# High and low halves of standing weights written element by element in turns

## The chip, the cores and the metric

The kernel runs on one core of one Trainium2 chip. The metric is device time in microseconds, from the start of the program to its end on that core.

## What is computed

The reference runs one network made of two blocks over 256 tokens of width 1024, all in fp32. Cut to what matters for the change:

```python
for l in range(2):                         # first block
    h, hc = norm(x) * (1 + sc1) + sh1, ... # latent tokens and context tokens
    u = h @ w_glu; q, k, v = h @ w_q, h @ w_k, h @ w_v; p = h @ w_p
    g = sigmoid(h @ w_g + b_gate)          # three gates of width 1024
    y = (g0 * y_a + g1 * y_b + g2 * y_c) @ w_out
    x = x + (silu(h2 @ w1) * (h2 @ w3)) @ w_ffn_out   # hidden width 2816
for i in range(2):                         # second block, on the same x
    x = x + concat(mixer(norm(x) @ w_in), memory) @ w_out
    x = x + (silu(g) * u) @ w_down         # g, u = split(norm(x) @ w_gate_up)
out = norm(x)
```

The first layer of the first block treats 256 latent and 256 context tokens together (512 columns), its second layer mostly the 256 latent ones, and the second block 256 tokens. Nearly all of the time goes into products of activations with weight matrices that are read once from memory.

## The kernel before, in words

The program is written engine by engine, with semaphores between the engines. `build` lays out the memory by hand; the first block is `block1`, the second `block2`.

To keep precision, each fp32 matrix is held as two fp32r halves: a high half, rounded, and a low half, the rest. `multiply` (L345 to L349) makes a product of three matmuls: first operand's high with second's high (L347), high with low (L348), low with high (L349). The first operand of a matmul stands still in the array and is fetched by a weight load of 128 x 128; the second moves through it.

Weights come in chunks of 1024 elements a partition. `T.load` (L256) books a chunk. SP's queue (`load_chunks`) brings it into the ring `raw` (3 buffers in the first block, 5 in the second). ScalarE copies it to the high half (L333), VectorE takes the high half off the raw chunk and so makes the low half (L336). Both do this in `split_until`, in the order in which TensorE uses the chunks, up to two chunks ahead. TensorE waits for `low_done` before it uses a chunk. A buffer of the split ring is filled again once TensorE has reported the last product that used it (`T.used`, `split_free`).

A split buffer is `[P, 2, SLOT]`: 1024 high elements, then 1024 low elements. The first block has 3 of them, the second 4. In the first block each exists twice over nearly the same memory: `level`, which starts at a multiple of 256 bytes as the activations HH and HL do, and `apart`, 64 bytes (`APART`) further. The second block has one set, 64 bytes past a multiple of 256. `T.load` chooses by the number of moving columns:

```python
two = rings[b][1 if columns > SEQ else 2][(len(old) - now["split"]) % SPLIT[b]]
```

Weights are used in two ways. Where the output is wanted with channels on the partitions, the weights stand still and the activations HH and HL move, 256 or 512 columns wide. This is so in `product_t`, `half_by_half`, `ffn_pe`, `raw_ffn_pe`, the gates and branches of the first block and the memory keys of the second. A chunk is then one output tile of 128 channels with 8 slices of the inner dimension (4 slices for two of the branches), so it takes 8 x 3 matmuls. A slice of the weights is 128 elements, 512 bytes, side by side. In `product` it is the other way round: the weights move, 512 or 256 columns wide, and the activations stand still.

In the profile, an operand pair such as `HH,apart` names the moving tile first and the standing one second; `split` is the `level` set in the first block and the only set in the second.

Of the kernel before, what the change touches and what calls it, by code (L numbers as in the profile page):

```python
# [123 lines left out]
def build(nc, A, out):  # L124
# [97 lines left out]
    class Tensor:  # L222
# [30 lines left out]
                milestones[key] = bank_no[1]  # L253
            ins.then_inc(pe_done, 1)

        def load(self, src, shape, split=True, ring="raw", home_free=None, split_home=None, later=False, columns=2 * SEQ):  # L256


            b = now["block"]
            mine = in_ring[ring]  # L260
            size = RAW[b] if ring == "raw" else MOD_RING
            s = (len(mine) - now[ring]) % size
            pieces = src if isinstance(src, list) else [src]
            loads[ring][s] += 16 * len(pieces)
            home = rings[b][0][s][:, :] if ring == "raw" else G[:, s, :]
            c = {"pieces": pieces, "shape": shape, "sem": slot_full[ring][s], "raw": view(home, shape), "full": loads[ring][s],
                 "free": None, "split": None, "before": mine[-size] if len(mine) - size >= now[ring] else None,
                 "mods": len(in_ring["mod"]) - len(held), "home_free": home_free}
            if later:
                held.append(c)  # L270
            else:
                chunks.append(c)
                chunks.extend(held)
                held.clear()
            mine.append(c)
            if not split:
                self.pe.wait_ge(c["sem"], c["full"])
                return c, c["raw"]
            k = c["split"] = len(splits)
            if split_home:  # L280
                two, c["split_free"] = split_home
            else:
                old = in_ring["split"]
                two = rings[b][1 if columns > SEQ else 2][(len(old) - now["split"]) % SPLIT[b]]
                c["split_free"] = old[-SPLIT[b]] if len(old) - SPLIT[b] >= now["split"] else None
                old.append(c)
            c["high"], c["low"] = view(two[:, 0, :], shape), view(two[:, 1, :], shape)
            splits.append(c)
            self.pe.wait_ge(low_done, k + 1)
            return c, (c["high"], c["low"])  # L290
# [16 lines left out]
    def view(t, shape):  # L307
        a, b = shape
        return t[:, 0:a * b].rearrange("p (a b) -> p a b", a=a)
# [51 lines left out]
    def product_t(T, pe, name, w, c0, tiles, kts, rhs, n, source=None, before=None, fill=None):  # L361

        per = SLOT // kts // P
        for j in range(tiles):
            if j % per == 0:
                src = source(j) if source else rows(w, 0, kts, c0 + j * P, per * P)
                i, ws = T.load(src, (kts, per * P), columns=n)
            if before:
                before(j)
            tile_t(T, pe, (name, j), ws, kts, j % per, rhs, n)  # L370
            if j % per == per - 1:
                T.used(i)
            if fill:
                fill(j)
# [703 lines left out]
    def half_by_half(T, pe, name, tiles, key, source, turned=0):  # L1078

        norm_pe(T, pe, name, tiles, turned, max(turned, 2))  # L1080
        norm_wait(pe, name, tiles[0:2])
        ws = {}
        for h in range(2):
            to = slice(h * SEQ, (h + 1) * SEQ)
            for p in range(3):
                if h == 0:
                    ws[p] = T.load(source(p), (KT, P), columns=SEQ)
                    T.open(key(p))
                for k in range(KT):
                    ins = multiply(pe, bank(key(p))[:, to], cut2(ws[p][1], slice(None), k), (HH[:, k, to], HL[:, k, to]), k == 0, k == KT - 1)  # L1090
                if h == 0 and p < 2:
                    norm_pe(T, pe, name, tiles, max(turned, 2 + p), 3 + p)
                elif h:
                    T.close(ins, key(p))
                    T.used(ws[p][0])
            if h == 0:
                norm_wait(pe, name, tiles)

    def ffn_pe(T, pe, L, w_up, w_down, tiles, n, U, wait, fill=nothing, down=nothing, last=1, homes=None, after_part=None):
        skip = 3 if len(tiles) > 2 else 0  # L1100
        parts = ("ffn_gate", 0), ("ffn_up", D_FF)
        if skip:
            half_by_half(T, pe, L + "n2", tiles, lambda p: (L + parts[p % 2][0], p // 2),
                         lambda p: rows(w_up, 0, KT, parts[p % 2][1] + p // 2 * P, P), 2)
        else:
            norm_pe(T, pe, L + "n2", tiles)
            keep_busy(T, pe, WARM_LAST[L + "n2"])
            wait(pe, L + "n2", tiles)
        for j in range(FT):
            for nm, c0 in parts:  # L1110
                if 2 * j + (nm == "ffn_up") < skip:
                    fill(2 * j + (nm == "ffn_up"))
                    continue
                i, ws = T.load(rows(w_up, 0, KT, c0 + j * P, P), (KT, P), columns=n)
                tile_t(T, pe, (L + nm, j), ws, KT, 0, both((HH, HL), n), n)
                T.used(i)
                fill(2 * j + (nm == "ffn_up"))
        product(T, pe, L + "ffn", w_down, FT, D, tiles, lefts(U), before=lambda k: pe.wait_ge(S(L + "hidden"), k + 1), fill=down, last=last,
                homes=homes, after_part=after_part)
# [86 lines left out]
    def _(pe):  # L1206
# [24 lines left out]
        for l in range(DEPTH):  # L1231
# [12 lines left out]

            for j in range(4):
                if j >= skip:
                    i, ws = T.load(rows(w_in, 0, KT, COL_P + j * P, P), (KT, P), columns=n)
                    tile_t(T, pe, (L + "pool", j), ws, KT, 0, own, n)
                    T.used(i)
                mod_pe(T, pe, L + "proj", j)  # L1250
                if j == 3 and l == 0:
                    for m in range(2):
                        turn_params(stage[1][:, m, :], ("cols", 1, m), 1)
                if j < 2 and first == 2:
                    norm_pe(T, pe, L + "n1", [0, 1, 2, 3], 2 + j, 3 + j)
            for j in range(NCH):
                for nm, c0 in glus:
                    i, ws = T.load(rows(w_in, 0, KT, c0 + j * P, P), (KT, P), columns=n)
                    tile_t(T, pe, (L + nm, j), ws, KT, 0, own, n)
                    T.used(i)  # L1260
                    mod_pe(T, pe, L + "proj", 4 + 2 * j + (nm == "glu"))
# [113 lines left out]

            def branch(name, number, gate_col, w, kts, pair, ready):
                for j in range(KT):
                    i, ws = T.load(rows(w_in, 0, KT, COL_G + gate_col * D + j * P, P), (KT, P), columns=n)
                    tile_t(T, pe, (name + "_gate", j), ws, KT, 0, own, n)
                    T.used(i)  # L1380
                    if number == 0 and l == 0 and j == 1:
                        conv_mean()
                    if number == 0 and l == 0 and j == 3:
                        conv_var()
                    if j == 0:
                        ready()
                    iy, wy = T.load(rows(w, 0, kts, j * P, P), (kts, P), columns=n)
                    tile_t(T, pe, (name, j), wy, kts, 0, both(pair, n), n)
                    T.used(iy)
                    if number == 1:  # L1390
                        gate_pe(T, pe, l, 0, j - 2)
# [823 lines left out]
    def raw_ffn_pe(T, pe, L, w_up, w_down, U, down):  # L2215

        raw_rows_pe(T, pe, L + "n2", 1)
        keep_busy(T, pe, BUSY_LAST)
        norm2_wait(pe, L + "n2", [0, 1])
        for j in range(FT):  # L2220
            for nm, c0 in (("ffn_gate", 0), ("ffn_up", D_FF)):
                i, ws = T.load(rows(w_up, 0, KT, c0 + j * P, P), (KT, P))
                tile_t(T, pe, (L + nm, j), ws, KT, 0, both((HH, HL), SEQ), SEQ)
                T.used(i)
                if j == 0 and nm == "ffn_gate":
                    spread_pe(T, pe, L + "n2")
        product(T, pe, L + "ffn", w_down, FT, D, [0, 1], lefts(U), before=lambda k: pe.wait_ge(S(L + "hidden"), k + 1), fill=down, last=2)
# [37 lines left out]
    def _(pe):  # L2265
# [3 lines left out]
        for e in range(DEPTH):  # L2269
# [56 lines left out]
            def next_memory(i):  # L2326
# [16 lines left out]
                if n < 2:  # L2343
                    key = ("E1_km", n)
                    if h == 0:
                        mem_chunks[n] = T.load(rows(w, 0, KT, n * P, P), (KT, P))
                        T.open(key, FILL_BANK)
                    c, ws = mem_chunks[n]
                    for k in range(4 * h, 4 * h + 4):
# [431 lines left out]
```

## Time and profile before

| | us |
|---|---|
| three runs | 2254.14, 2245.88, 2249.35 |
| median | 2249.35 |
| the profiled execution | 2247.56 |
| its span, first to last instruction | 2245.8 |
[...]

The profile shows one execution. PE are matmuls and PEld the weight loads beside them. A matmul's record holds its whole passage through the array, longer than the interval to the next one, so the pace is read from counts in windows without idle time, not from the mean of one. Where the rows give a mean, a longer one for the same form still says that it was held up.

### The profile page before, as it was taken

The numbers are of one execution on the slowest core, as the hardware profiler recorded it, in microseconds if no ns is written. First come the engines' busy times: TensorE is split into PE (matmuls) and PEld (weight loads), VectorE is DVE, ScalarE is ACT, GpSimd is POOL, SyncE is SP. The second block draws the span as 40 slices with busy tenths as digits, with TensorE's granted clock in tenths as the row PEclk, the third lists the DMA queues.
The fourth block names the chain that finished last, engine by engine and source line by source line (L and its number), as shares of the span: only waits on it lengthen the run. The fifth ranks groups of instructions, "written<-read, shape, count | busy, mean of one in ns | idle before, by whom it ended". The sixth has DMA issues, their size and how long they took to land. (4 is left out here: it accounts for less than half of the span.)

```text
span 2245.8 us, 32948 instructions
## 1 busy us (share of the span) xinstructions
PE 2160.7 (96%) x13134; PEld 1870.9 (83%) x13134; DVE 1444.3 (64%) x2148; ACT 888.4 (40%) x1389; POOL 179.5 (8%) x251
## 2 busy tenths in 40 slices
PE   5999999999999999999999999999999999999998
PEld 3777667878888888788886998998888998898997
DVE  3587685664467667237967776874785665566664
ACT  3322373332342212235327545443544444444443
POOL 3422000000000000004310001000100000000000
PEclk9999999999999999999999999999989999999999
DMA  8544302333335566234420565776633666543663
GB/s 281 160 141 141 99 1 62 96 97 94 113 103 170 177 197 207 99 116 139 129 75 24 170 181 160 238 215 194 160 113 90 184 187 195 155 130 113 188 196 123
DMA packets 428653, 320.81 MB, mean 143 GB/s; under 512 B 25925, under 2 KB 379702, under 8 KB 428502
## 3 DMA queue, kind: packets, MB, share of 16 engines
q1 hardware_dynamic: 425408, 310.52, 45.8%
q0 software_dynamic: 2656, 8.03, 1.2%
q8 instruction: 105, 1.72, 0.3%
q14 instruction: 46, 0.38, 0.0%
q10 hardware_dynamic: 438, 0.17, 0.0%
HBM read 317.62 MB, written 1.05 MB: 142 GB/s over the span
## 5 line engine op out<-in xcount | busy, mean ns | idle before, releaser
L336 DVE TENSOR_TENSOR split<-raw,split 128x1024 fp32r<-128x1024 f32 (+1 forms) x382 | 460.2, 1209 | 366.8 <-ACT split L333 365.9
L347 PE MATMUL PS<-HH,split 128*128 128x256 f32 (+1 forms) x1752 | 590.9, 337 | 4.1 <-DVE HL L2163 1.7
L349 PE MATMUL PS<-HH,split 128*128 128x256 f32 (+1 forms) x1752 | 580.0, 331 | 0.0
L348 PE MATMUL PS<-HL,split 128*128 128x256 f32 (+1 forms) x1752 | 579.9, 331 | 0.0
L333 ACT ACTIVATE split<-raw 128x1024 fp32r<-128x1024 f32 (+1 forms) x382 | 389.1, 1033 | 359.8 <-PE PS L349 324.4
L347 PEld LDWEIGHTS PS<-HH,split 128*128 128x128 f32 x1752 | 331.3, 189 | 42.2 <-issue 9.0
L348 PEld LDWEIGHTS PS<-HL,split 128*128 128x128 f32 x1752 | 334.1, 191 | 32.0 <-issue 1.0
L349 PEld LDWEIGHTS PS<-HH,split 128*128 128x128 f32 x1752 | 331.0, 189 | 31.6
L347 PE MATMUL PS<-HH,apart 128*128 128x256 f32 x800 | 227.0, 284 | 17.8 <-DVE HL L487 11.8
L348 PE MATMUL PS<-HL,apart 128*128 128x256 f32 x800 | 223.2, 279 | 0.0
L349 PE MATMUL PS<-HH,apart 128*128 128x256 f32 x800 | 223.1, 279 | 0.0
L336 DVE TENSOR_TENSOR apart<-raw,apart 128x1024 fp32r<-128x1024 f32 x118 | 136.4, 1162 | 69.4 <-ACT apart L333 68.8
L347 PEld LDWEIGHTS PS<-HH,apart 128*128 128x128 f32 x800 | 152.0, 190 | 22.0 <-DVE HL L487 13.3
L347 PE MATMUL PS<-split,UH 128*128 128x512 f32 x416 | 165.3, 397 | 1.4 <-DVE split L336 1.4
L348 PE MATMUL PS<-split,UH 128*128 128x512 f32 x416 | 162.6, 391 | 0.0
L349 PE MATMUL PS<-split,UL 128*128 128x512 f32 x416 | 162.4, 390 | 0.0
L1744 DVE SCALAR_TENSOR_TENSOR CV<-UP,cols,CV 128x512 f32<-128x512 f32 (+1 forms) x240 | 155.1, 708 | 0.2
L348 PEld LDWEIGHTS PS<-HL,apart 128*128 128x128 f32 x800 | 152.0, 190 | 0.2
L349 PEld LDWEIGHTS PS<-HH,apart 128*128 128x128 f32 x800 | 152.1, 190 | 0.0
L333 ACT ACTIVATE apart<-raw 128x1024 fp32r<-128x1024 f32 x118 | 117.4, 999 | 82.6 <-PE PS L349 54.2
L938 DVE SCALAR_TENSOR_TENSOR XN<-G,silu_c,XN 128x1024 f32<-128x1024 f32 x70 | 88.0, 1281 | 36.0 <-ACT UT L1127 35.3
L347 PEld LDWEIGHTS PS<-split,UH 128*128 128x128 f32 x416 | 78.4, 189 | 19.2 <-DVE split L336 2.0
(339 smaller groups left out, 3117.9 us busy)
## 6 DMA issues: line engine op xcount, KB each, us to landing
raw<-in_w_in_dram SPq DMA_DIRECT2D x120, 512.0 KB, 4.2
raw<-in_w_ffn_in_dram SPq DMA_DIRECT2D x88, 512.0 KB, 4.8
raw<-in_l_w_gate_up_dram SPq DMA_DIRECT2D x88, 512.0 KB, 3.9
G<-in_w_mod_dram SPq DMA_DIRECT2D x82, 512.0 KB, 3.9
raw<-in_w_ffn_out_dram SPq DMA_DIRECT2D x44, 512.0 KB, 3.5
raw<-in_l_w_down_dram SPq DMA_DIRECT2D x44, 512.0 KB, 4.5
raw<-in_l_w_in_dram SPq DMA_DIRECT2D x28, 512.0 KB, 3.9
raw<-in_w_attn_out_dram SPq DMA_DIRECT2D x16, 512.0 KB, 4.3
```

The lines of the kernel that those rows point to most:

```text
L333: eng.activation(c["high"], c["raw"], ACT.Copy).then_inc(high_done, 1)
L336: eng.tensor_tensor(c["low"], c["raw"], c["high"].bitcast(F32), ALU.subtract).then_inc(low_done, 1)
L347: pe.matmul(out, a[0], b[0], start=first, stop=False)
L348: pe.matmul(out, a[0], b[1], start=False, stop=False)
L349: return pe.matmul(out, a[1], b[0], start=False, stop=last)
L938: ins = dve.scalar_tensor_tensor(at, c["raw"][:, 0, :], s, at, ALU.mult, ALU.add)
L1744: ins = dve.scalar_tensor_tensor(CV[:, j, 0:ns, :], src, wt, CV[:, j, 0:ns, :], ALU.mult, ALU.add)
```

## The change

`T.load` gets an argument `still` in place of `columns`. For a chunk whose weights stand still, the split buffer is taken from the `apart` set whatever the number of moving columns, and the two halves are laid out in turns: high element 0, low element 0, high element 1, and so on. The high view and the low view then have a step of two elements, 8 bytes. ScalarE writes every second element, VectorE reads and writes every second element, and a weight load reads 128 elements out of 1024 bytes. Chunks that move keep two halves one behind the other, in the `level` set.

```diff
-        def load(self, src, shape, split=True, ring="raw", home_free=None, split_home=None, later=False, columns=2 * SEQ):
+        def load(self, src, shape, split=True, ring="raw", home_free=None, split_home=None, later=False, still=False):
...
-                two = rings[b][1 if columns > SEQ else 2][(len(old) - now["split"]) % SPLIT[b]]
+                two = rings[b][2 if still else 1][(len(old) - now["split"]) % SPLIT[b]]
...
-            c["high"], c["low"] = view(two[:, 0, :], shape), view(two[:, 1, :], shape)
+            if still:
+                a, n = shape
+                pairs = two.rearrange("p o (n h) -> p (o n) h", h=2)
+                c["high"], c["low"] = (pairs[:, 0:a * n, h].rearrange("p (a n) -> p a n", a=a) for h in range(2))
+            else:
+                c["high"], c["low"] = view(two[:, 0, :], shape), view(two[:, 1, :], shape)
...
-                i, ws = T.load(src, (kts, per * P), columns=n)
+                i, ws = T.load(src, (kts, per * P), still=True)
...
-                i, ws = T.load(rows(w_up, 0, KT, c0 + j * P, P), (KT, P), columns=n)
+                i, ws = T.load(rows(w_up, 0, KT, c0 + j * P, P), (KT, P), still=True)
```

The same last edit is made in `half_by_half`, at the pool and gated-unit tiles, at the gates and branches of the first block, in `raw_ffn_pe` and at the memory keys: everywhere weights stand still.

## Rows read from the trace of the kernel before

**Rows 1.** Busy time, share of the span and instructions of each engine, from the page.
```profile
PE 2160.7 (96%) x13134; PEld 1870.9 (83%) x13134; DVE 1444.3 (64%) x2148; ACT 888.4 (40%) x1389; POOL 179.5 (8%) x251
```

**Rows 2.** TensorE's waits: us in total, times, longest.
```profile
PE PS L347 <- DVE HL L487: 11.8, 4, 8.3
...
PE PS L347 <- DVE apart L336: 7.1, 7, 3.2
...
PE PS L347 <- DVE split L336: 1.4, 1, 1.4
...
PE PS L703 <- DVE split L336: 0.9, 1, 0.9
```

**Rows 3.** Matmuls in windows: length, busy us (count), granted clock, DMA share, GB/s.
```profile
1410.00:1480.00 70.00, 70.00 (x620) 1.00 0.82 246
1780.00:1850.00 70.00, 70.00 (x597) 1.00 0.65 188
2100.00:2170.00 70.00, 70.00 (x596) 1.00 0.65 186
955.00:990.00 35.00, 35.00 (x156) 1.00 0.34 107
```

**Rows 4.** Forms in the windows 1410:1500 (`apart`) and 1770:1890 (`split`): busy, mean ns.
```profile
L348 PE MATMUL PS<-HL,apart 128*128 128x256 f32 x260 | 71.8, 276 | 0.0
...
L348 PEld LDWEIGHTS PS<-HL,apart 128*128 128x128 f32 x260 | 48.8, 188 | 0.0
...
L348 PE MATMUL PS<-HL,split 128*128 128x256 f32 x294 | 82.6, 281 | 0.0
...
L348 PEld LDWEIGHTS PS<-HL,split 128*128 128x128 f32 x294 | 56.4, 192 | 0.0
```

**Rows 5.** Weight loads in order of time, 1484.5:1485.7: start, length.
```profile
1484.33 1.31 PEld L917 LDWEIGHTS PS<-ones,XN 128*128 128x128 f32 x11
1485.56 0.19 PEld L347 LDWEIGHTS PS<-HH,apart 128*128 128x128 f32 x1
```

**Rows 6.** Matmuls by form, whole span: count, busy, mean ns.
```profile
L348 PE MATMUL PS<-HL,split 128*128 128x512 f32 x784 | 307.8, 393 | 0.0
...
L348 PE MATMUL PS<-HL,split 128*128 128x256 f32 x968 | 272.1, 281 | 0.0
...
L348 PE MATMUL PS<-HL,apart 128*128 128x256 f32 x800 | 223.2, 279 | 0.0
...
L348 PE MATMUL PS<-OTL,apart 128*128 128x256 f32 x64 | 18.5, 289 | 0.0
```

**Rows 7.** Matmuls by form in the windows 1000:1595 and 400:450.
```profile
L348 PE MATMUL PS<-HL,apart 128*128 128x256 f32 x704 | 195.6, 278 | 0.0
...
L348 PE MATMUL PS<-HL,split 128*128 128x512 f32 x48 | 18.7, 389 | 0.0
```

**Rows 8.** The two split lines: their forms, then their busy time in two windows.
```profile
L333 ACT ACTIVATE split<-raw 128x1024 fp32r<-128x1024 f32 x363 | 377.0, 1053 | 359.8 <-PE PS L349 324.4 <-DVE X L2174 8.9 <-DMA raw<-in_w_in_dram 8.2
...
L336 DVE TENSOR_TENSOR split<-raw,split 128x1024 fp32r<-128x1024 f32 x363 | 446.6, 1234 | 324.0 <-ACT split L333 323.1
...
1410.00:1480.00 70.00, 27.52 (x26) 1.00 0.82 246
...
1410.00:1480.00 70.00, 31.12 (x26) 1.00 0.82 246
1780.00:1850.00 70.00, 29.66 (x25) 1.00 0.65 188
```

**Rows 9.** All engines in two windows: PE, PEld, DVE, ACT, POOL, granted clock, DMA share, GB/s.
```profile
1410.00:1500.00 90.00, 90.00 (x796) 90.00 (x796) 73.53 (x105) 39.73 (x50) 0.00 (x0) 1.00 0.79 233
1770.00:1890.00 120.00, 120.00 (x955) 117.22 (x954) 79.74 (x119) 50.15 (x63) 0.00 (x0) 1.00 0.65 192
```

**Rows 10.** VectorE in order of time, 1780:1790, with the idle time before.
```profile
1782.50 1.22 DVE L336 TENSOR_TENSOR split<-raw,split 128x1024 fp32r<-128x1024 f32 x1 [1.43 <-ACT split L333]
1783.64 0.41 DVE L2246 TENSOR_TENSOR UT<-UT,PS 128x256 f32<-128x256 f32 x1
1784.09 0.30 DVE L340 CAST UH<-UT 128x256 fp32r<-128x256 f32 x1
1784.42 0.42 DVE L341 TENSOR_TENSOR UL<-UT,UH 128x256 fp32r<-128x256 f32 x1
1784.76 1.22 DVE L336 TENSOR_TENSOR split<-raw,split 128x1024 fp32r<-128x1024 f32 x1
```

More of the change, by code:

```diff
@@ L1086, in half_by_half @@
                 if h == 0:
-                    ws[p] = T.load(source(p), (KT, P), columns=SEQ)
+                    ws[p] = T.load(source(p), (KT, P), still=True)
                     T.open(key(p))
@@ L1246, in _ @@
                 if j >= skip:
-                    i, ws = T.load(rows(w_in, 0, KT, COL_P + j * P, P), (KT, P), columns=n)
+                    i, ws = T.load(rows(w_in, 0, KT, COL_P + j * P, P), (KT, P), still=True)
                     tile_t(T, pe, (L + "pool", j), ws, KT, 0, own, n)
@@ L1257, in _ @@
                 for nm, c0 in glus:
-                    i, ws = T.load(rows(w_in, 0, KT, c0 + j * P, P), (KT, P), columns=n)
+                    i, ws = T.load(rows(w_in, 0, KT, c0 + j * P, P), (KT, P), still=True)
                     tile_t(T, pe, (L + nm, j), ws, KT, 0, own, n)
@@ L1377, in branch @@
                 for j in range(KT):
-                    i, ws = T.load(rows(w_in, 0, KT, COL_G + gate_col * D + j * P, P), (KT, P), columns=n)
+                    i, ws = T.load(rows(w_in, 0, KT, COL_G + gate_col * D + j * P, P), (KT, P), still=True)
                     tile_t(T, pe, (name + "_gate", j), ws, KT, 0, own, n)
@@ L1386, in branch @@
                         ready()
-                    iy, wy = T.load(rows(w, 0, kts, j * P, P), (kts, P), columns=n)
+                    iy, wy = T.load(rows(w, 0, kts, j * P, P), (kts, P), still=True)
                     tile_t(T, pe, (name, j), wy, kts, 0, both(pair, n), n)
@@ L2221, in raw_ffn_pe @@
             for nm, c0 in (("ffn_gate", 0), ("ffn_up", D_FF)):
-                i, ws = T.load(rows(w_up, 0, KT, c0 + j * P, P), (KT, P))
+                i, ws = T.load(rows(w_up, 0, KT, c0 + j * P, P), (KT, P), still=True)
                 tile_t(T, pe, (L + nm, j), ws, KT, 0, both((HH, HL), SEQ), SEQ)
@@ L2345, in next_memory @@
                     if h == 0:
-                        mem_chunks[n] = T.load(rows(w, 0, KT, n * P, P), (KT, P))
+                        mem_chunks[n] = T.load(rows(w, 0, KT, n * P, P), (KT, P), still=True)
                         T.open(key, FILL_BANK)
```

## Prediction

> **What bounds the kernel now.** I read the shares of the engines first. The reader is to see that TensorE is busy for 96% of the span and its weight loads for 83%, VectorE for 64% and ScalarE for 40% [rows 1]. The table of waits by engine comes next: TensorE waits 7.1, 1.4 and 0.9 us for a low half, which is all the time in which it stood for want of split weights [rows 2]. So the order of work ends with TensorE, and the change counts by what it does to the pace at which weight loads and matmuls follow each other.
>
> That pace I read from windows without any idle time. Two matmuls at most are already under way where a window opens, so I take two off each count. The 70 us from 1410 (second layer's hidden layer, 256 moving columns, loads from `apart`) hold 618 matmuls, 113.3 ns each. The 70 us from 1780 and from 2100 (same shapes, second block) hold 595 and 594, 117.7 ns each [rows 3]. Nothing in the instruction differs. The same form takes 276 ns there and 281 ns here, and one of the three loads in a turn takes 192 instead of 188 ns [rows 4]. So there are two paces, and the slow one costs 4.4 ns a matmul. With 512 moving columns, 154 in 35 us give 227 ns, twice the quick pace [rows 3]: 113.3 ns is what 256 moving columns need by themselves.
>
> A weight load has a pace too. Where a matmul has one moving column, eleven loads start in 1485.56 - 1484.33 = 1.23 us, 111.8 ns each [rows 5]. A matmul of 256 columns therefore leaves its load 1.5 ns to spare, one of 512 columns 115 ns. This is the number on which the change hangs.
>
> **The change part by part.** It adds no instruction, wait or transfer, and removes none. No buffer changes its size, and the rings, their counts and the order of SP's queue stay as they are. Three things differ for a chunk whose weights stand still.
>
> (1) Its weight load reads 128 elements out of 1024 bytes instead of 512. How many matmuls that touches: `split` with 256 columns 968 a line, `apart` 800 and 64 a line, over three lines 5496, and the branches of four slices some 200 more (estimated from the loop: 2 x 8 tiles x 4 slices x 3), together 5690 with 256 columns [rows 6]. With 512 columns it is some 2500 (784 a line and the small groups) [rows 6]; there a load may grow by 115 ns before it is felt, and I cost them at nothing.
>
> The trace has no load or other operand that reads every second element, so I bound its price. From below: the load stays at 111.8 ns, and TensorE no longer meets the slow pace. All of the second block's matmuls at the quick one is 3 x 968 x 4.4 ns = 12.8 us. In the first block the mean between 1000 and 1595 is 278 ns, two fifths of the way from 276 to 281, so 3 x 704 x 0.4 x 4.4 = 3.7 us, and 3 x 96 x 4.4 = 1.3 us for the rest if all of it is slow [rows 6, 7]. Together 18 us, as the most that can be had, since 113.3 ns stays the floor of the moving columns and stalls also stand in that mean. From above: the load takes twice its time because it covers twice the bytes, 224 ns, and 5690 x (224 - 113.3) ns - 18 us = 612 us are lost. Between them stands one row. The moving operand covers 1024 bytes in 113.3 ns [rows 3]; a load that reads its 1024 bytes as fast ends just when its matmul does. It is the nearest row, because it is the same engine reading the same length of the same memory, and I take it. Then the load is neither late nor early, and which of the two paces TensorE falls into stays open, as the trace shows no cause for it but how a stretch began. I leave the shares as they are: 0 us, with 18 us of gain and, if all goes at 117.7 ns, 5690 x 4.4 - 18 = 7 us of loss on the two sides.
>
> [...]
>
> [...]
>
> (2) ScalarE writes the high half with gaps, VectorE reads it with gaps and writes the low half with gaps. These splits take 1.05 us (ScalarE) and 1.23 us (VectorE) a chunk [rows 8]. No row has fp32 elements at every second place. Below: no change. Above: both double. I take no change: the nearest rows are the same instructions on a contiguous chunk, and both engines move as many elements as before. What hides them: ScalarE is busy 27.5 of 70 us with splits, VectorE 31.1 of 70 us with splits [rows 8] and 73.5 of 90 us with everything [rows 9]. If the cover is gone, VectorE needs 73.5 + 90 / 70 x 31.1 = 113.5 us in those 90, that is 26% longer, and 79.7 + 120 / 70 x 29.7 = 130.6 in the 120 us of the second block, 9% longer [rows 9]. The stretches last 22 pairs of chunks, 5.44 us a pair (48 x 113.3) and twice 5.65 us, so 22 x (5.44 x 0.26 + 2 x 5.65 x 0.09) = 53 us.
>
> (3) Chunks with 512 moving columns move from `level` to `apart`, 64 bytes further. At 227 ns they are at the floor of their moving columns with either [rows 3], and their means of 393 ns against the floor's 389 [rows 6, 7] leave 2500 x 4 ns = 10 us, most of it halved clock and stalls. I take 0.
>
> The sum: 0 + 0 + 0, with the profiled execution at 2247.56 us, of which its span is 2245.8 and 1.8 lie around it. It lies 1.8 us under the median of the three runs, 2249.35. I say 2248.
>
> **The rivals.** 0.5%, 11 us, is about what a measurement of this kernel can tell from no change.
> A: freed. Weights and moving columns now pass through memory at the same pace, 64 bytes apart, so they never meet and the quick pace is the only one. For it: the slow pace exists, and it comes with a longer load [rows 4]. Against it: the first block holds the quick pace for 70 us with loads as they are [rows 3], so distance in memory alone doesn't make the slow one. It gives 2249 - 18 to 2249 - 11, 2231 to 2238 us. More isn't to be had.
> B: the load becomes the bound, in TensorE's 256-column stretches. It decides from 113.3 ns on, 1.5 ns above what it takes now. [...] At 120 ns it is +20 us, 2269. At half as much again, 168 ns, it is 5690 x 54.7 ns - 18 us = +293 us, 2542. Twice is 2861. For it: only 1.5 ns of cover. Against: a moving operand covers as much at 113.3.
> [...]
> C: ScalarE and VectorE slow down, VectorE becomes the bound: up to +53 us, 2302. Against it: idle time before every second split, 1.43 us long [rows 10].
> D: nothing is seen, because 512-column matmuls hide it and 256-column ones keep their mix. This is my forecast.
>
> **How the numbers follow.** D 0.39, A 0.28, B small (from 2260 to 2285) 0.17, B large 0.10, C 0.06. Faster is A, same is D, slower is B and C, 0.33. The range leaves out B large, half of C and the end of A: 2232 to 2280. As cases of both signs hold most of the chance, D's own range is 2240 to 2258.
>
> **What would show it.** In the window of 1410, a form mean of 276 ns and 618 matmuls in 70 us if the load is still hidden. In the second block's hidden layers, 276 instead of 281 ns for A, 281 for D. For B, loads that follow at more than 113.3 ns with matmuls of the same interval, and 512-column matmuls still at 227. For C, means above 1.05 and 1.23 us on the two split lines and waits of TensorE for a low half. I am wrong if the load's own price is not near that of the moving columns, or if weights and columns that pass at the same pace always meet and not never.

## The result and the profile after

| | before | changed |
|---|---|---|
| median, us | 2250.19 (4 runs, 2245.88 to 2254.14) | 2274.32 (4 runs, 2270.03 to 2281.09) |
| the profiled execution, us | 2247.56 | 2281.09 |
| its span, us | 2245.8 | 2279.3 |
| mean granted TensorE clock | 0.985 | 0.982 |

The ratio is 1.0106, with a 95% interval from 1.007 to 1.0142: the changed kernel is slower, by 24 us in the medians, where no change had been forecast. The time lies inside the range, 2232 to 2280. The profiled execution is the longest of its four, 6.8 us above their median; the other three have clocks of 0.985 to 0.987.

In the changed kernel the three matmuls of `multiply` stand in L352, L353 and L354, ScalarE's half of the split in L338 and VectorE's in L341. The shares on the profile's page of the changed kernel, beside [rows 1]:

```profile
PE 2196.7 (96%) x13134; PEld 1916.4 (84%) x13134; DVE 1445.5 (63%) x2148; ACT 920.1 (40%) x1389; POOL 177.8 (8%) x251
```

TensorE grew by 36.0 us, its weight loads by 45.5, ScalarE by 31.7, VectorE by 1.2. So the loss is TensorE's own, and what is left to ask is which matmuls carry it. The same windows as in [rows 3], changed kernel, and ahead of them one in the first layer of the first block, where weights stand still under 512 moving columns:

```profile
420.00:440.00 20.00, 20.00 (x88) 1.00 0.32 93
955.00:990.00 35.00, 35.00 (x156) 1.00 0.30 98
1410.00:1480.00 70.00, 70.00 (x583) 1.00 0.75 224
1780.00:1850.00 70.00, 70.00 (x585) 1.00 0.65 191
2100.00:2170.00 70.00, 70.00 (x585) 1.00 0.63 183
```

The first of these in the kernel before:

```profile
420.00:440.00 20.00, 20.00 (x90) 1.00 0.32 90
```

All 256-column stretches with standing weights now have one pace: 583 to 585 matmuls in 70 us, which less two is 120.1 to 120.5 ns, against 620, 597 and 596. Where weights move (955:990), nothing changed. Under 512 columns 88 matmuls fit where 90 did. The forms of the window 1410:1500 show the load beside its matmul, to be set against 276 and 188 ns in [rows 4] (busy, mean ns; before, all three loads of a turn took 188 ns there):

```profile
L353 PE MATMUL PS<-HL,apart 128*128 128x256 f32 x250 | 70.9, 284 | 0.0
...
L354 PEld LDWEIGHTS PS<-HH,apart 128*128 128x128 f32 x250 | 48.9, 196 | 0.0
```

The whole span by forms, against [rows 6]: 393 became 396 ns with 512 columns, 279 became 286 in the first block, and 281 stayed 281 on this line of the second:

```profile
L353 PE MATMUL PS<-HL,apart 128*128 128x512 f32 x784 | 310.2, 396 | 0.0
...
L352 PE MATMUL PS<-HH,split 128*128 128x256 f32 x968 | 278.1, 287 | 3.1 <-DVE HL L2168 1.7 <-DVE HL L645 0.8 <-DVE RT L713 0.5
...
L353 PE MATMUL PS<-HL,split 128*128 128x256 f32 x968 | 272.2, 281 | 0.0
L353 PE MATMUL PS<-HL,apart 128*128 128x256 f32 x800 | 228.5, 286 | 0.0
```

A mean of one form hides a loss that is spread over the three of a turn, so I took the time from each matmul's start to the next one's from the trace, left out every gap of 135 ns or more (260 ns with 512 columns), which are stalls or the halved clock (a granted clock of 0.50, as from 895.4 to 898.6 us in the kernel before), and summed what is over the floor of 113.3 (226.7) ns:

| matmuls with standing weights | before: mean ns, us over the floor | changed | difference, us |
|---|---|---|---|
| 2784 with 256 columns, first block | 114.3, 2.7 | 120.0, 17.9 | 15.2 |
| 2904 with 256 columns, second block | 117.4, 11.7 | 120.0, 19.1 | 7.4 |
| 2736 with 512 columns | 227.3, 1.6 | 230.5, 10.2 | 8.6 |

That is 31.2 of the 33.5 us by which the two spans differ, and the matmuls whose weights move stay within 0.1 us of where they were. The medians differ by less, 24 us, with an interval from 16 to 32 (0.7 and 1.42% of 2250). The idle time of TensorE shrank from 85.1 to 82.6 us (span less busy), which gives a little back.

The splits in the whole span, changed kernel:

```profile
L338 ACT ACTIVATE split<-raw 128x1024 fp32r<-128x1024 f32 x257 | 276.4, 1099 | 210.6 <-PE PS L354 192.0 <-DVE X L2179 8.9 <-DVE X L2176 4.8
L338 ACT ACTIVATE apart<-raw 128x1024 fp32r<-128x1024 f32 x208 | 239.0, 1151 | 219.2 <-PE PS L354 188.8 <-DMA raw<-in_w_in_dram 21.8 <-DMA raw<-in_w_ffn_in_dram 8.5
...
L341 DVE TENSOR_TENSOR split<-raw,split 128x1024 fp32r<-128x1024 f32 x257 | 313.5, 1225 | 259.9 <-ACT split L338 259.6
```

And TensorE's wait for a low half, from the table of waits (us, times, longest):

```profile
PE PS L352 <- DVE apart L341: 5.9, 6, 3.1
```

ScalarE's copy went from 1053 ns [rows 8] to 1099 and 1151, VectorE's subtraction stayed where it was, and TensorE waits no longer for a low half than in [rows 2]. ScalarE's 32 us are hidden.

### The profile page after: what moved, and what is told of

It is laid out like the page before. It is cut to its first block and busy times, and to the rows that moved or that the text cites. A ratio compares the mean times of both kernels' runs of the same rounds, so it can differ in the third digit from the quotient of the medians.

```text
span 2279.3 us, 32948 instructions
## 1 busy us (share of the span) xinstructions
PE 2196.7 (96%) x13134; PEld 1916.4 (84%) x13134; DVE 1445.5 (63%) x2148; ACT 920.1 (40%) x1389; POOL 177.8 (8%) x251
## 5 line engine op out<-in xcount | busy, mean ns | idle before, releaser
L352 PE MATMUL PS<-HH,apart 128*128 128x256 f32 (+1 forms) x1584 | 550.3, 347 | 17.1 <-DVE HL L492 11.7
L353 PE MATMUL PS<-HL,apart 128*128 128x256 f32 (+1 forms) x1584 | 538.6, 340 | 0.0
L354 PE MATMUL PS<-HH,apart 128*128 128x256 f32 (+1 forms) x1584 | 537.7, 339 | 0.0
L341 DVE TENSOR_TENSOR split<-raw,split 128x1024 fp32r<-128x1024 f32 x260 | 316.0, 1221 | 259.9 <-ACT split L338 259.6
L341 DVE TENSOR_TENSOR apart<-raw,apart 128x1024 fp32r<-128x1024 f32 x240 | 280.5, 1171 | 195.4 <-ACT apart L338 194.7
L338 ACT ACTIVATE split<-raw 128x1024 fp32r<-128x1024 f32 x260 | 278.7, 1095 | 210.6 <-PE PS L354 192.0
L352 PEld LDWEIGHTS PS<-HH,apart 128*128 128x128 f32 x1584 | 312.3, 197 | 52.2 <-DVE HL L492 13.2
L338 ACT ACTIVATE apart<-raw 128x1024 fp32r<-128x1024 f32 x240 | 259.9, 1086 | 223.5 <-PE PS L354 193.1
L353 PEld LDWEIGHTS PS<-HL,apart 128*128 128x128 f32 x1584 | 312.0, 197 | 29.0 <-issue 1.2
L354 PEld LDWEIGHTS PS<-HH,apart 128*128 128x128 f32 x1584 | 312.2, 197 | 28.8
L352 PE MATMUL PS<-HH,split 128*128 128x256 f32 x968 | 278.1, 287 | 3.1 <-DVE HL L2168 1.7
L354 PE MATMUL PS<-HH,split 128*128 128x256 f32 x968 | 273.8, 283 | 0.0
L353 PE MATMUL PS<-HL,split 128*128 128x256 f32 x968 | 272.2, 281 | 0.0
L352 PEld LDWEIGHTS PS<-HH,split 128*128 128x128 f32 x968 | 187.8, 194 | 6.7 <-issue 4.5
L353 PEld LDWEIGHTS PS<-HL,split 128*128 128x128 f32 x968 | 189.2, 195 | 0.2
L354 PEld LDWEIGHTS PS<-HH,split 128*128 128x128 f32 x968 | 188.5, 195 | 0.0
L352 PE MATMUL PS<-split,UH 128*128 128x512 f32 x416 | 165.2, 397 | 1.4 <-DVE split L341 1.4
L353 PE MATMUL PS<-split,UH 128*128 128x512 f32 x416 | 162.5, 391 | 0.0
L354 PE MATMUL PS<-split,UL 128*128 128x512 f32 x416 | 162.4, 390 | 0.0
L352 PEld LDWEIGHTS PS<-split,UH 128*128 128x128 f32 x416 | 78.5, 189 | 19.1 <-DVE split L341 2.0
```

What stands on the lines that cost most here:

```text
L338: eng.activation(c["high"], c["raw"], ACT.Copy).then_inc(high_done, 1)
L341: eng.tensor_tensor(c["low"], c["raw"], c["high"].bitcast(F32), ALU.subtract).then_inc(low_done, 1)
L352: pe.matmul(out, a[0], b[0], start=first, stop=False)
L353: pe.matmul(out, a[0], b[1], start=False, stop=False)
L354: return pe.matmul(out, a[1], b[0], start=False, stop=last)
```

## The experiments

Three theories could give 120 ns. Theory 1: the load of every second element is itself longer than its matmul. Theory 2: load and moving columns meet in memory, in a way that depends on their distance. Theory 3: the splits, writing with gaps, disturb TensorE's reads.

**A table of paces.** A program of its own runs the same pattern of three matmuls a slice with nothing beside it: weights as two contiguous halves (`cols`), in turns (`turns`), in turns by slices of 128 (`slices`), at every third or fourth element, each at several offsets from a multiple of 256 bytes, where the activations lie.

```diff
+        if kind == "c":
+            f = lambda h, k: t[:, 1024 * h + 128 * k:1024 * h + 128 * (k + 1)]
+        elif kind == "s":
+            f = lambda h, k: t[:, 256 * k + 128 * h:256 * k + 128 * (h + 1)]
+        else:
+            v = t.rearrange("p (n h) -> p n h", h={"i": 2, "t": 3, "d": 4}[kind])
+            f = lambda h, k: v[:, 128 * k:128 * (k + 1), h]
```

> A program of its own, with none of the reference's work: TensorE runs four tiles of 8 x 3 fp32r matmuls for each of many layouts of the standing weights (halves one behind the other, in turns by element, in turns by slice of 128, every third and every fourth element), at offsets of 0 to 224 bytes against the moving columns, with 256, 512 and 8 moving columns, each twice. Afterwards ScalarE and VectorE write with and without gaps, alone and beside TensorE. Read is the interval between matmuls. Theory 1 (the load itself takes longer): with 8 moving columns, loads of every second element follow at about 120 ns, against 112 for contiguous ones, and the interval with 256 columns is 120 at every offset; with 512 columns it stays 227. Theory 2 (load and moving columns meet in memory): with 8 columns both follow at 112 ns, with 256 columns the interval depends on the offset, some at 113 and some at 118 to 121, and with 512 columns there are a few ns over 227 for turns alone. Theory 3 (writes of the other engines with gaps disturb TensorE): in this program, turns without other engines run at 113 ns, and above it only beside them. [...] ScalarE's write with gaps some 100 ns longer than 1.05 us in all theories.

Mean ns from start to start with 256 columns, each run of 96 matmuls seen twice with at most 1.5 ns between the two. One of the sixteen second runs, `cols` at 0, fell into the halved clock (0.50) and is left out. The table gives the first:

| offset, bytes | 0 | 32 | 64 | 96 | 128 | 160 | 192 | 224 |
|---|---|---|---|---|---|---|---|---|
| cols | 119.9 | 118.4 | 113.3 | 117.3 | 118.6 | 120.0 | 117.8 | 116.7 |
| turns | 120.1 | 120.0 | 120.0 | 120.7 | 120.0 | 120.0 | 121.7 | 120.0 |

Slices in turns give 120.0 at 0 and 113.4 at 64; every third element gives 173.3, every fourth 235.5. Windows of this program, matmuls: `cols` at 0, `turns` at 0, `cols` at 64, `turns` at 64, every third, every fourth.

```profile
30.00:38.00 8.00, 8.00 (x69) 1.00 0.01 2
42.00:51.00 9.00, 9.00 (x77) 1.00 0.01 2
77.00:86.00 9.00, 9.00 (x81) 1.00 0.01 2
88.00:98.00 10.00, 10.00 (x86) 1.00 0.01 2
...
240.00:252.00 12.00, 12.00 (x71) 1.00 0.00 1
257.00:274.00 17.00, 17.00 (x74) 1.00 0.00 0
```

For contiguous halves the interval changes with the offset, for turns hardly: turns are at 120 or a little more even where the contiguous halves are at their best. Each run stands behind two or three matmuls of 128 columns, and what stands in front turns out below to matter for contiguous halves. With 512 columns, contiguous halves take 226.7 at 0 and 233.4 at 64, turns 233.3 and 230.0. Windows at 0 (`cols`, `turns`) and 64 (`cols`, `turns`):

```profile
280.00:300.00 20.00, 20.00 (x90) 1.00 0.00 0
302.00:322.00 20.00, 20.00 (x87) 1.00 0.00 1
325.00:345.00 20.00, 20.00 (x88) 1.00 0.00 1
347.00:367.00 20.00, 20.00 (x88) 1.00 0.00 1
```

So the numbers of the changed kernel, 120.0 and 230.5, come out with no other engine at work, and they stay the same beside ScalarE and VectorE writing with gaps (contiguous halves 113.3 ns by the middle interval, turns 120.0 in the mean). Theory 3 falls. ScalarE alone shows its own price (least, middle, most ns; contiguous, then mostly with gaps):

```profile
L166 ACT ACTIVATE D<-X x5: 1056/1056/1056, 1009.8 to 1014.2; 128x1024 fp32r<-128x1024 f32 x5
```
```profile
L166 ACT ACTIVATE D<-X x7: 1056/1115/1117, 1015.3 to 1022.1; 128x1024 fp32r<-128x1024 f32 x7
```

VectorE's subtraction takes 1226 ns either way. The runs with 8 moving columns, meant to show the load without its matmul, came out at 213 ns for nearly all layouts because the granted clock had fallen to 0.50 in them; they tell nothing and were made anew below.

**The offset alone.** The kernel before, with the ring chosen as in the change but the halves left contiguous:

```diff
-                two = rings[b][1 if columns > SEQ else 2][(len(old) - now["split"]) % SPLIT[b]]
+                two = rings[b][2 if still else 1][(len(old) - now["split"]) % SPLIT[b]]
```

> The changed kernel with contiguous halves again: of the change only the 64 bytes of offset for chunks with 512 moving columns are left. If the turns cause it all (theories 1, 2, 3): 2250 us, as before, and 227 ns with 512 columns. If the offset of the 512-column chunks has a part: up to 8 us above before, with 229 to 234 ns there.

It took 2265.15 us (12 runs) against 2249.6 (23 runs), ratio 1.0073, interval 1.0038 to 1.0108. Windows under 512 columns and in the first block's hidden layer:

```profile
420.00:440.00 20.00, 20.00 (x87) 1.00 0.32 93
...
1410.00:1480.00 70.00, 70.00 (x614) 0.99 0.79 238
```

Nearly all of the loss lies with the 512-column matmuls, 233.4 ns instead of 227.3: 16.0 us over all of them, twice the 8 us that the expectation allowed. Those with 256 columns lost 1.8 us. The prediction's third step, taken at nothing, costs as much in time when it is made alone as the turns for 256 columns do in the next run, 2265.15 and 2264.94 us.

**Turns for 256 columns only.** The changed kernel, with 512-column chunks put back:

```diff
+            still = still and not wide
...
-                i, ws = T.load(src, (kts, per * P), still=True)
+                i, ws = T.load(src, (kts, per * P), still=True, wide=n > SEQ)
```

> The changed kernel with the turns only for chunks with up to 256 moving columns; those with 512 are contiguous and in the ring without offset, as before. The mean interval with 512 columns rose from 227.3 to 230.3 ns for 2500 matmuls, 8 us. Theory 2 (each part disturbs by itself): 2274 - 8 = 2266 us, and 256-column matmuls stay at 120 ns. Theory 1: the same time for 256 columns, but then it has no account of the 8 us. If the 512-column part costs nothing: 2274.

It took 2264.94 us (12 runs), ratio 1.0063, interval 1.0042 to 1.0084:

```profile
420.00:440.00 20.00, 20.00 (x90) 1.00 0.33 99
...
1410.00:1480.00 70.00, 70.00 (x585) 1.00 0.75 227
```

Its 256-column matmuls lie 37.2 us over the floor instead of 14.4. Of these 22.8 us the profiled execution is longer by 17.6: the long intervals that the sums leave out, stalls and halved clock, are 5 us less.

**Turns for 512 columns only.** The other half of the same cut:

```diff
-            if still:
+            if still and wide:
```

> The changed kernel with the turns only for chunks with 512 moving columns; those with up to 256 are contiguous at the offset, as before. It is the counterpart of the run with the turns for up to 256 columns. If the two parts add: 230.5 instead of 227.3 ns for 2736 matmuls, 9 us above before, 2259 us, with 114 to 117.5 ns for 256 columns. If the parts don't add (one hides the other): before's time, or the changed kernel's.

It took 2256.43 us (12 runs) against 2251.3 (17 runs), ratio 1.0031, interval 1.0001 to 1.006. Under 512 columns the pace is 230.1 ns, 7.5 us more in sum than before:

```profile
420.00:440.00 20.00, 20.00 (x89) 1.00 0.39 113
...
1410.00:1480.00 70.00, 70.00 (x597) 1.00 0.77 230
1780.00:1850.00 70.00, 70.00 (x597) 1.00 0.65 188
```

The window at 1410 brought something not asked for: its loads and buffers are those of the kernel before, yet it runs at the slow pace, 597 and not 620, which puts 4.8 us more over the floor in the first block. In the trace the two halves add up, 22.8 us with 256 columns in the one and 7.5 with 512 in the other, beside 22.6 and 8.6 in the whole. The times say less. Their 0.63 and 0.31% make 0.94, inside the whole's 0.7 to 1.42, but the 0.31 has those 4.8 us in it, and its profiled execution has 8 us less in long intervals than the one before, at a mean granted clock of 0.990 against 0.985.

**Turns without the offset.** The changed kernel with every split buffer at a multiple of 256 bytes:

```diff
-            line_up(at_h + APART)
+            line_up(at_h)
...
-                two = rings[b][2 if still else 1][(len(old) - now["split"]) % SPLIT[b]]
+                two = rings[b][1][(len(old) - now["split"]) % SPLIT[b]]
```

> The changed kernel with the turns kept and the 64 bytes of offset taken away, in both blocks (all chunks start at a multiple of 256 bytes like the activations). Theory 1: 120 ns with 256 columns as with the offset, 2274 us. Theory 2: another interval than 120 with 256 columns and than 230 with 512; worse if meeting is now constant (above 125 ns, 2300 us and more), better if 64 bytes happened to be the bad distance (113 to 118, 2240 to 2262).

It took 2286.3 us (4 runs), ratio 1.0158, interval 1.0114 to 1.0201:

```profile
420.00:440.00 20.00, 20.00 (x87) 1.00 0.32 93
...
1410.00:1480.00 70.00, 70.00 (x581) 0.99 0.74 224
1780.00:1850.00 70.00, 70.00 (x584) 1.00 0.66 191
```

With 256 columns the pace is 119.99 ns in both blocks: for turns the offset doesn't matter there. With 512 columns it is 233.3 instead of 230.5. The second block's moving weights lost too, 233.3 instead of 226.9 ns in 671 matmuls of 512 columns. Their ring had lost its 64 bytes, while the activations that stand still under them there (`UH` and `O2H` in the profile) still lie, by the kernel's layout, 64 bytes past a multiple of 256. In the first block, where these activations and the moving weights both lie at a multiple of 256, the moving weights kept 227.3.

**The load by itself.** A second program, in which 48 matmuls of 512 columns stand before each burst of 24 with 128 or 8 moving columns (granted clock 1.00 in the bursts shown below, where the runs with 8 columns above had 0.50), and further bursts for the two paces:

```diff
+            between("wide", 4)
+            for tag, kind, dists, n, tiles, pre in RUNS:
+                between(*pre)
+                run(mm[tag], [weights(kind, x) for x in dists], n, tiles)
```

> A second program of its own, without the reference's work. It sends loads of each layout beside 128 and 8 moving columns for one tile at a time, each behind two tiles with 512 columns so that the clock is still at its upper level. Theory 1 (a load of every second element is itself longer): contiguous loads follow at 111.7 ns, those of every second element at 120, of every third at 173, of every fourth at 235. Theory 2 (it is only longer where columns move beside it): the first two at 111.7 ns. Then 512 moving columns with both layouts at offsets of 0 to 224 bytes: contiguous at 0 is the only one at 226.7 ns if distance decides. Last, contiguous halves at the very distances of the two blocks' rings (three buffers of the first, four of the second, and the second's spread by 256 bytes each) behind twelve kinds of instruction: if the slow pace of the second block (117.7 ns) comes from where its buffers lie, it shows at 'second' behind all of them and not at 'first' or 'spread'; if it comes from how a stretch begins, it changes with the instruction in front and is the same for the three.

| every ... element | 1st | slices in turns | 2nd | 3rd | 4th |
|---|---|---|---|---|---|
| bytes covered by a load | 512 | 512 | 1024 | 1536 | 2048 |
| beside 128 columns, ns | 111.6 | 111.6 | 120.0 | 175.5 | 233.5 |
| beside 8 columns, ns | 111.6 | 111.7 | 117.8 | 173.3 | 233.3 |

Windows of weight loads inside four of the bursts with 128 columns (1st, 2nd, 3rd, 4th), all at full clock:

```profile
55.40:57.40 2.00, 1.96 (x19) 1.00 0.00 0
82.60:85.00 2.40, 2.40 (x21) 1.00 0.00 0
137.40:141.00 3.60, 3.60 (x22) 1.00 0.02 5
170.80:175.60 4.80, 4.80 (x22) 1.00 0.00 0
```

One is under way where a window opens: 20 in 2.40 us are 120 ns, 21 in 4.80 us 229. I take 117.8 ns, beside eight columns, as the load's own: contiguous loads stay at 111.6 beside either number of columns. That is already longer than the 113.3 ns of the moving columns, so theory 1 holds for 256 columns. The last 2.2 ns, up to 120.0, come only beside 128 or more columns; what they are is not shown. At 1024, 1536 and 2048 bytes the load goes by the bytes that it covers, 117.8 / 1024 = 0.115, 173.3 / 1536 = 0.113 and 233.3 / 2048 = 0.114 ns a byte. At 512 it is 111.6 ns, 0.218 a byte.

It can't hold for 512 columns, where the load has 107 ns to spare. There the same program gives, by offset from 0 to 224 in steps of 32, for contiguous halves 226.7, 233.3, 233.4, 234.3, 232.4, 233.3, 229.0, 233.3 (the first by its middle value) and for turns 233.3, 232.2, 230.0, 233.3, 231.5, 235.7, 233.3, 233.4. Windows for turns at 32, contiguous at 64 and turns at 64:

```profile
390.00:398.00 8.00, 8.00 (x36) 1.00 0.00 0
400.00:409.00 9.00, 9.00 (x40) 1.00 0.00 0
412.00:421.00 9.00, 9.00 (x41) 1.00 0.00 0
```

The length of the load doesn't explain these. Its place matters, as theory 2 has it; that the two meet in memory is argued from this and not shown. For contiguous halves it is the place against the other operand that counts. The second block's moving weights run at 226.9 ns with both operands 64 bytes past a multiple of 256, and at 233.3 when their ring alone moves to the multiple (turns without the offset, above). Why an equal place is the one without loss for 512 columns, and 64 bytes apart the best for 256, is open.

The same program asks where the second block's slow pace comes from. It lays contiguous buffers out as in the first block, as in the second, and spread; and puts different instructions in front of stretches of up to 192 matmuls. Behind one matmul of 128 columns the second block's layout runs at 117.8 and the first's at 113.4. Behind one of 512 columns, all three layouts run at 113.3. Behind eight with one column, all three at 117.8. Of the twelve fronts, five gave the quick pace to all three layouts (three matmuls of 128 columns, four transposes, one or two of 512 columns, nothing), two the slow one to all (two of 128 columns, eight with one), and with five it differed by layout. So neither of the expectation's two cases came out whole: it isn't the second block's layout alone, nor the front alone. Windows for the second block's and then the first's layout behind one of 128 columns, and for the second's behind one of 512 (from 961.9 on the first's, at the same pace):

```profile
570.00:590.00 20.00, 20.00 (x172) 1.00 0.01 2
593.00:608.00 15.00, 15.00 (x135) 1.00 0.00 1
```
```profile
946.00:966.00 20.00, 20.00 (x177) 1.00 0.00 1
```

So the slow pace is something that TensorE falls into at the start and keeps, with the same buffers and the same instructions. It is settled by what ran in front together with the layout. All three layouts lie 64 bytes past a multiple of 256, so the 113.3 ns of that offset in the table of paces isn't owed to the offset alone: behind two matmuls of 128 columns single buffers at 64 ran at 113.3 and these layouts at 117.8. Whether the other offsets of that table would run quicker behind another front was not tried. The expectation for the next two runs counts eighteen quick stretches out of eighteen. The trace has fifteen behind a 512-column matmul, behind nothing, or behind three or four short ones of 128 columns, and behind three matmuls with one column two of three layouts were slow.

**The pace set, and spoilt.** Two kernels made from the one before. In `pace_set` two 512-column matmuls stand in front of each hidden layer of the second block and behind the matmul that interrupts it; in `pace_spoilt` one 128-column matmul stands in front of a hidden layer in the first block.

```diff
+    def set_pace(T, pe, n):
+        ps = T.open(("busy",), (BANKS - 1,))
+        for i in range(n):
+            ins = pe.matmul(ps[:, 0:2 * SEQ], HH[:, 0, 0:P], HH[:, 0, :], start=True, stop=True)
+        ins.then_inc(bank_read[BANKS - 1], 1)
...
         norm2_wait(pe, L + "n2", [0, 1])
+        set_pace(T, pe, 2)
```

> The kernel before, with two fp32r matmuls of 512 moving columns more in front of each hidden layer of the second block, and two behind the spread matmul that interrupts it. In the program of its own, eighteen stretches out of eighteen that followed such a matmul or another stretch in the quick pace, or three or four short ones, ran at 113.3 ns, and most behind one or two short matmuls at 117.8, whatever the address. Theory (the pace is a state that the instruction in front sets, and that lasts): the windows of the second block's hidden layers hold 618 matmuls in 70 us instead of 595, a form mean of 276 instead of 281 ns, 2 x 44 x 24 x 4.4 ns = 9.3 us less against 8 x 0.23 = 1.8 us more: 2242 beside 2250. Rival (the second block's buffers or its other engines hold the slow pace): 117.7 ns as before and 2252.

```diff
+            if j == 0 and n == SEQ:
+                ps = T.open(("busy",), (BANKS - 1,))
+                ins = pe.matmul(ps[:, 0:P], HH[:, 0, 0:P], HH[:, 0, 0:P], start=True, stop=True)
+                ins.then_inc(bank_read[BANKS - 1], 1)
```

> The kernel before, with one fp32r matmul of 128 moving columns more in front of the hidden layer of the first block's second layer, which ran at 113.3 ns. Theory of the state: behind one short matmul the stretch from 1400 to 1520 may run at 117.8 ns, up to 44 x 24 x 4.4 ns = 4.6 us slower, 2255 beside 2250. Rival (addresses): 113.3 ns as before, 2250.

`pace_set` has the quick pace in both stretches of the second block, against 597 and 596 in [rows 3]:

```profile
1780.00:1850.00 70.00, 70.00 (x620) 1.00 0.68 196
2100.00:2170.00 70.00, 70.00 (x620) 1.00 0.67 194
```

Its matmuls of the second block are 2.3 us over the floor instead of 11.7. It took 2244.96 us against 2248.76 (12 and 23 runs), ratio 0.9986, interval 0.9954 to 1.0018. The 9.4 us in the intervals, less some 1.8 for the eight matmuls added (estimated in the expectation), can be read from the trace, but in the time they can't be told from nothing. `pace_spoilt` missed: its stretch kept the quick pace, and its time is the same as before (2248.88, ratio 1.0002, 0.9971 to 1.0032). The window that was to become slow:

```profile
1410.00:1480.00 70.00, 70.00 (x620) 1.00 0.81 246
```

One 128-column matmul doesn't bring on the slow pace there, as it didn't in the first block's layout of the second program. So a front that gives the quick pace is shown in the kernel itself, one that takes it away is not.

## Why the prediction was wrong

**Step 1, 256 columns: the term that was mis-sized.** The load of every second element was taken at 113.3 ns, as fast as the moving operand covers the same 1024 bytes, and so at no cost. The kind of reasoning held: from 1024 bytes on the load goes by the bytes that it covers, at 0.113 to 0.115 ns a byte, where the moving operand has 113.3 / 1024 = 0.111. But the load of every second element measured 117.8 ns by itself and 120.0 beside the moving columns. The value chosen had used up the cover of 1.5 ns, so the 6.7 ns of error are all loss. The prediction's own rival B (small) had it: at 120 ns +20 us for all 256-column matmuls, and the trace has 15.2 + 7.4 = 22.6 over 5688 of them. It was given 0.17, because the value chosen was itself exactly the threshold. A best estimate that lies on the threshold says that both sides are near even, and here the gain side was capped and the loss side wasn't.

By itself the load of every second element took 117.8 ns against 111.6 for the contiguous one, and those of every third and fourth took 173.3 and 233.3 ns (`load_alone`): none of those that cover more than 512 bytes was free.

**Step 1, 512 columns: the reasoning itself was wrong.** They were costed at nothing because the load has 115 ns to spare. It has 107 even at 120 ns, and the 2736 of them (the prediction had some 2500) lost 8.6 us all the same, 3.2 ns each. The offset alone, with contiguous loads of 111.6 ns (`load_alone`) hidden under intervals of 227.3, took 6.1 ns a matmul and 16.0 us. So a hidden load can still go with a slower matmul above it, by where it reads; through what, no run shows.

**Step 3, the move to `apart`, taken at 0.** Alone it costs 233.4 - 227.3 = 6.1 ns a matmul and 16 us. Turns at that place soften it to 230.5. The argument, that they are at the floor with either set, rested on a window at 227 ns [rows 3] in which the weights move, and on a form whose weights stand still in `level` [rows 6]. In both, the operands lie at the same place within 256 bytes, and so they do in the second block, where weights and standing activations both lie 64 past. No row had the two operands of a 512-column matmul 64 bytes apart. With contiguous halves that distance gave 233.3 to 233.4 ns each time: standing weights in the offset alone and in both programs, moving ones in the run of turns without the offset. An equal place gave 226.7 to 227.3.

**Step 2, the splits, taken at no change: right in effect.** ScalarE's copy costs 46 to 98 ns more than 1053, well below the doubled bound, and is hidden. VectorE's costs nothing (1226 ns either way), and VectorE was to carry rival C, so C falls.

**Rival A and the forecast D.** The time lies inside the wide range because B's small version was let in. Of D's own range, 2240 to 2258, it is outside. That the slow pace could vanish or stay was the wrong question for this change, since 120 ns lies above both. A took the slow pace for a meeting in memory that distance would cure. The same buffers ran at 113.3 and 117.8 ns behind different instructions, so distance alone doesn't decide, as the prediction held against it. Before the change, 2.7 + 11.7 = 14.4 us lay over the floor, where the prediction had capped the gain at 18.

What stays open: what in the instructions ahead sets the pace, why the stretch at 1410 turned slow when only earlier chunks had changed, where the load of turns gets its last 2.2 ns, and why a few distances are free and the others are not.

## What to carry to other kernels

Where TensorE is the bound with 256 moving columns, a weight load has about 1.5 ns of cover (113.3 less 111.8), and none of the three layouts that widened it was free here (120.0, 173.3 and 235.5 ns for every second, third and fourth element): keep standing weights contiguous within a slice (slices of 128 in turns kept 113.4 ns at 64 bytes), and measure a load's own time beside few columns before costing it at nothing. A change that moves a buffer should have its offset against the other operand tested by itself, also where the load is well hidden. Compare the distance between the two operands, not the address of one (moving weights of 512 columns: 226.9 ns with both operands 64 bytes past a multiple of 256, 233.3 with one). When the best estimate of an unknown cost is the very number from which it decides, split the chances by what each side can still bring, and don't call it zero.

## What the runs showed of the hardware that was not expected

- A load of 128 fp32 weights takes 111.6 ns with 512 bytes covered and some 0.114 ns a byte with 1024, 1536 and 2048 (117.8, 173.3, 233.3 ns, all in `load_alone` beside eight columns).
- With 512 moving columns and contiguous standing weights, the interval is 226.7 ns where both lie at a multiple of 256 bytes, and 229.0 to 234.3 at the seven other offsets of 32 bytes (`load_alone`). With moving weights it is 226.9 where both lie 64 bytes past such a multiple (the kernel before), and 233.3 where only the standing operand does (`turns_no_offset`).
- With 256 columns and contiguous standing weights it is the other way round: behind two or three matmuls of 128 columns, 113.3 ns only at 64 bytes past such a multiple (also at 320, 576, 832 and 1088, `load_alone`), 116.7 to 120.0 elsewhere (`pace_table`).
- The same 192 matmuls run at 113.3 or 117.8 ns each, from the first to the last, by what TensorE did just before (`load_alone`, the second block's layout behind one matmul of 512 or of 128 columns).
- ScalarE writes 1024 fp32 elements with gaps in 1115 ns instead of 1056. VectorE's subtraction takes 1226 either way (`pace_table`).
